# Summing the later adaLN columns on VectorE instead of TensorE in a hybrid decoder layer

## What is computed

```
mod = silu(c) @ w_ada + b_ada          # w_ada: 1024 x 6144
sh_m, sc_m, gt_m, sh_f, sc_f, gt_f = split(mod, 6)
h = rmsnorm(x, norm_pre_mix) * (1 + sc_m) + sh_m
proj = h @ w_in                        # 1024 x 4168
o = concat(hgrn2(4 heads of proj), sparse attention(4 heads, top 128 of 512 keys by an indexer))
x = x + gt_m * rmsnorm(o @ w_out, norm_post_mix)
h = rmsnorm(x, norm_pre_ffn) * (1 + sc_f) + sh_f
gate, up = split(h @ w_ffn_in, 2)      # 1024 x 5632
x = x + gt_f * rmsnorm((silu(gate) * up) @ w_ffn_out, norm_post_ffn)
```

## Time and profile before

| | us |
|---|---|
| median of 3 runs (802.88 to 803.44) | 803.05 |
| profiled execution, its own time | 805.04 |
| its span, first to last instruction | 803.3 |
| busy: TensorE / VectorE / ScalarE | 758.8 / 408.1 / 283.4 |

### The profile page before, as it was taken

How to read it: one execution, slowest core, us unless ns; L and a number is a source line. 1 busy time by engine, 2 the same in 40 slices (tenths; PEclk the granted TensorE clock), 3 DMA queues, 4 the chain that set the end, 5 groups by cost and what they waited for, 6 DMA issues and landing times.

```text
span 803.3 us, 10163 instructions
## 1 busy us (share of the span) xinstructions
PE 758.8 (94%) x3554; PEld 584.6 (73%) x3554; DVE 408.1 (51%) x782; ACT 283.4 (35%) x463; POOL 11.4 (1%) x39
## 2 busy tenths in 40 slices
PE   4889999999999889998997999999999999999995
PEld 3555477777866576665885888888888888888884
DVE  3857669797988525427347332222333225344344
ACT  6345452534233233244257233322233333112123
POOL 5000000000000000000000000000000000000000
PEclk9899999999999989997998999999999999999998
DMA  9935015243343150552410432233333233423202
GB/s 310 347 88 150 1 45 167 73 136 102 106 134 107 28 179 19 165 204 84 160 50 27 131 100 84 80 102 104 104 104 91 77 94 123 139 80 103 78 1 105
DMA packets 103845, 88.02 MB, mean 110 GB/s; under 512 B 2980, under 2 KB 93192, under 8 KB 103816
## 3 DMA queue, kind: packets, MB, share of 16 engines
q1 hardware_dynamic: 103816, 87.65, 35.6%
HBM read 85.55 MB, written 2.10 MB: 109 GB/s over the span
## 4 chain that ended last, share of the span: by engine, by line
PE 84%; DVE 9%; issue 2%; DMA 2%; ACT 1%; SPq 1%; DVEq 0%; ACTq 0%
PE ps L1240 45%; PE ps L1261 21%; PE ps L1346 3%; PE ps L1453 2%; PE ps L1291 2%; PE ps L1521 1%; PE ps L1431 1%; DMA w_raw<-in_w_in 1%; DVE w_lo L779 1%; PE ps L1496 1%; PE ps L1580 1%; PE ps L1516 1%; PE ps L1588 1%; DVE score L1002 1%; DVE top L997 1%
## 5 line engine op out<-in xcount | busy, mean ns | idle before, releaser
L1240 PE MATMUL ps<-h_hi,w_hi 128*128 128x512 f32 x576 | 235.2, 408 | 1.1 <-DVE h_lo L832 1.1
L1240 PE MATMUL ps<-h_hi,w_lo 128*128 128x512 f32 x576 | 225.1, 391 | 0.0
L1240 PE MATMUL ps<-h_lo,w_hi 128*128 128x512 f32 x576 | 225.0, 391 | 0.0
L779 DVE TENSOR_TENSOR w_lo<-w_raw,w_hi 128x1024 fp32r<-128x1024 f32 (+1 forms) x110 | 128.7, 1187 | 168.8 <-ACT w_hi L434 168.6
L434 ACT ACTIVATE w_hi<-w_raw 128x1024 fp32r<-128x1024 f32 (+1 forms) x110 | 110.5, 1026 | 97.4 <-PE ps L1261 91.7
L1240 PEld LDWEIGHTS ps<-h_hi,w_hi 128*128 128x128 f32 x576 | 108.5, 188 | 43.5 <-issue 21.7
L1240 PEld LDWEIGHTS ps<-h_hi,w_lo 128*128 128x128 f32 x576 | 108.4, 188 | 23.6
L1240 PEld LDWEIGHTS ps<-h_lo,w_hi 128*128 128x128 f32 x576 | 108.7, 189 | 20.5 <-issue 1.0
L1261 PE MATMUL ps<-w_hi,h_hi 128*128 128x512 f32 x240 | 94.8, 395 | 0.8 <-DVE mix L1138 0.8
L1261 PE MATMUL ps<-w_lo,h_hi 128*128 128x512 f32 x240 | 94.0, 392 | 0.0
L1261 PE MATMUL ps<-w_hi,h_lo 128*128 128x512 f32 x240 | 93.9, 391 | 0.0
(11 more groups left out here) (223 smaller groups left out, 696.6 us busy)
## 6 DMA issues: line engine op xcount, KB each, us to landing
w_raw<-in_w_ffn_in SPq DMA_DIRECT2D x44, 512.0 KB, 4.0
w_raw<-in_w_in SPq DMA_DIRECT2D x28, 512.0 KB, 6.4
w_raw<-in_w_ffn_out SPq DMA_DIRECT2D x22, 512.0 KB, 3.6
adaw<-in_w_ada SPq DMA_DIRECT2D x20, 512.0 KB, 5.0
act<-in_w_ada SPq DMA_DIRECT2D x12, 512.0 KB, 9.0
res<-in_x SPq DMA_DIRECT2D x8, 512.0 KB, 4.8
adaw<-in_w_ada SPq DMA_DIRECT2D x4, 1024.0 KB, 5.3
act<-in_w_ada SPq DMA_DIRECT2D x4, 1024.0 KB, 5.2
```

What stands on the lines that cost most here:

```text
L779: V.tensor_tensor(w_lo[slot][:, 0:n], w_raw[slot][:, 0:n], w_hi[slot][:, 0:n].bitcast(f32), ALU.subtract).then_inc(lo_ok, 1)
L1240: last = mm(ps[bank][0:rows, :], a, b, start=(k == 0 and n == 0), stop=(k == KT - 1 and n == 2))
```

## The change

The sum over the 1024 rows is taken apart. VectorE holds a running total of 128 partitions x 1024 columns for each later block. For row block k (128 rows, one per partition) it adds w_ada[k rows, 1024 columns] times silu(c) of these rows, a per-partition scalar (scalar_tensor_tensor). After eight adds, the total only has to be summed over partitions, which TensorE does with ones: for the gates one matmul of ones with the total both sums and spreads (gate_rows), for shift and scale 16 small ones make columns (ffn_sums).

- HGRN2 heads: halves, sums, copies and bias adds are gone.
- Attention heads 0, 1, 2: VectorE does eight adds each, for gt_m, sh_f, sc_f: two at t = 2, two after the last normalise, four after the copy of the output to mix. Loads are 1 MB (two row blocks), in two slots; twelve in all.
- The diagonals with L1135, L1588, L702 and the wait of head 1 for them are gone. The bias of a gate is loaded into row 0 of the total, which POOL has zeroed; the post-norm gains are loaded spread over all partitions instead of with the small parameters (two small loads fewer at the start).
- Attention head 3: ahead of its output matmuls TensorE does gate_rows for gt_m and ffn_sums; VectorE multiplies the gates by the gain.
- FFN: gt_f is summed in passes 0 to 7, one 512 KB load and one add each (add_tail), the loop of passes is cut in two, and gate_rows stand before the last pass.

The core of the diff:

```
@@ SP
-            load_gates_ada(0, 0)
...
-            load_norm_ada(3, 1)
+            def load_sum(n):
+                col = (2, 3, 4)[n // 4] * D_MODEL
+                if n == 0:
+                    sp.wait_ge(ada_used, START_ADA)
+                elif n == 1:
                     sp.wait_ge(o_mm, HG_HEADS)
                 else:
+                    sp.wait_ge(sum_used, 2 * n - 2)
+                sp.dma_start(sum_slot[n % 2].rearrange("p (k n) -> p k n", k=2),
+                             w_ada_k[:, 2 * (n % 4):2 * (n % 4) + 2, col:col + D_MODEL]).then_inc(sum_loaded[n % 2], 16)
+            def load_tail(k):
+                wait_apart(sum_used, k + SUMS)
+                sp.dma_start(tail_slot, w_ada[0][ds(k * P, P), 5 * D_MODEL:6 * D_MODEL]).then_inc(tail_loaded, 16)
...
+            with sp.Fori(0, KT) as i:
+                load_fin(i)
+                load_tail(i)
+            with sp.Fori(KT, FT // 2) as i:
+                load_fin(i)
@@ VectorE
+            def add_sum(h, n):
+                ve.wait_ge(sum_loaded[n // 2 % 2], h * 32 + 16 * (n // 4 + 1))
+                w = sum_slot[n // 2 % 2][:, n % 2 * D_MODEL:(n % 2 + 1) * D_MODEL]
+                silu = silu_pad[:, n * 32:n * 32 + 1]
+                first_head = isinstance(h, int)
+                total = sum_gate_mix if first_head else act[:, ds(h * D_MODEL, D_MODEL)]
+                if n == 0 and first_head:
+                    ve.wait_ge(mix_bias, 16)
+                else:
+                    ve.wait_ge(sum_used, h * KT + n)
+                if n == 0 and not first_head:
+                    V.tensor_scalar(total, w, silu, None, ALU.mult).then_inc(sum_used, 1)
+                else:
+                    V.scalar_tensor_tensor(out=total, in0=w, scalar=silu, in1=total, op0=ALU.mult,
+                                           op1=ALU.add).then_inc(sum_used, 1)
+            def add_tail(k):
+                ve.wait_ge(tail_loaded, k * 16 + 16)
+                V.tensor_copy(silu_k[:, :], silu_pad[:, ds(k * 32, 1)]).then_inc(tail_k, 1)
+                ve.wait_ge(tail_k, k + 1)
+                ve.wait_ge(sum_used, k + SUMS)
+                V.scalar_tensor_tensor(out=sum_gate_ffn, in0=tail_slot, scalar=silu_k[:, :], in1=sum_gate_ffn,
+                                       op0=ALU.mult, op1=ALU.add).then_inc(sum_used, 1)
@@ VectorE, att_body
+                    if not last and t == 2:
+                        add_sum(h, 0)
+                        add_sum(h, 1)
+                    if not last and t == 2:
                         split_lo(h * 3 + (G_ATT + 5), 2)
                 normalise(TT - 1)
                 if not last:
+                    add_sum(h, 2)
+                    add_sum(h, 3)
+                if not last:
                     split_lo(h * 3 + (G_ATT + 6), 0)
-                adaln_set(h)
-                if first:
...
-                    for n in range(2 * KT):
-                        V.tensor_scalar(diag[:, n * P:(n + 1) * P], ident[:, :], gate_cols[:, n:n + 1], None,
-                                        ALU.mult).then_inc(diag_ok, 1)
+                if last:
+                    ve.wait_ge(post_loaded, 32)
+                    for b in range(2):
+                        ve.wait_ge(gate_mm, b + 1)
+                        V.tensor_tensor(gate_mix[:, b * SEQ:(b + 1) * SEQ], ps[2 + b][:, :],
+                                        gate_mix[:, b * SEQ:(b + 1) * SEQ], ALU.mult).then_inc(gate_ok, 1)
+                    ve.wait_ge(ada_sum, 1)
+                    V.tensor_tensor(mod[:, 24:40], ps[6][:, 0:16], prm[:, 24:40], ALU.add).then_inc(mod_ok, 1)
                 ve.wait_ge(pv_mm, h * 4 + 4)
                 V.tensor_copy(mix[:, ds(h * SEQ + HG_HEADS * SEQ, SEQ)], ps[7][:, :]).then_inc(att_out, 1)
+                if not last:
+                    for n in range(4, KT):
+                        add_sum(h, n)
@@ TensorE
-                        ada_half(5, st // 2, adaw)
-                    elif st == 7:
-                        te.wait_ge(rows_ok, h + 1)
-                        ada_sums(5)
...
+            def gate_rows(total, bank, b):
+                mm(ps[bank + b][:, :], ones[:, :], total[:, b * SEQ:(b + 1) * SEQ], start=True,
+                   stop=True).then_inc(gate_mm, 1)
+            def ffn_sums():
+                for n in range(2 * KT):
+                    total = (sum_shift, sum_scale)[n // KT]
+                    last = mm(ps[6][:, n:n + 1], total[:, n % KT * P:(n % KT + 1) * P], ones[:, 0:1], start=True,
+                              stop=True)
                 last.then_inc(ada_sum, 1)
@@ TensorE, att_body
                 if not first:
-                    te.wait_ge(gate_ok, 4)
-                    te.wait_ge(mod_ok, h + (HG_HEADS + 1))
+                    te.wait_ge(v_ok, h)
                 partner(0, aq)
...
                 fill(20, 24)
+                if last:
+                    te.wait_ge(sum_used, SUMS)
+                    te.wait_ge(lg_ok, TT * ATT_HEADS)
+                    gate_rows(sum_gate_mix, 2, 0)
+                    gate_rows(sum_gate_mix, 2, 1)
+                    ffn_sums()
                 for t in range(TT):
-                    if t == TT - 1:
-                        te.wait_ge(rows_ok, h + (HG_HEADS + 1))
-                        ada_sums(6)
@@ TensorE, FFN
+            te.wait_ge(sum_used, SUMS + KT)
+            gate_rows(sum_gate_ffn, 4, 0)
+            gate_rows(sum_gate_ffn, 4, 1)
             fin_pass(FT // 2 - 1, False, True)
```

More of the change, by code:

```diff
@@ L171, in build @@
         small = sem("small")
[L172 removed]
+        sum_loaded, sum_used = [sem(f"sum_loaded{n}") for n in range(2)], sem("sum_used")
+        mix_zero, ffn_zero, mix_bias, ffn_bias = (sem(n) for n in ("mix_zero", "ffn_zero", "mix_bias", "ffn_bias"))
+        post_loaded, tail_loaded, tail_k = sem("post_loaded"), sem("tail_loaded"), sem("tail_k")
         ada_used, mod_ok, scale_ok = sem("ada_used"), sem("mod_ok"), sem("scale_ok")
@@ L290, in load_out @@
                 load_rows(w_out, k, k % 4)
[L292 to L305, removed]
+            w_ada_k = w_ada[0].rearrange("(k p) n -> p k n", p=P)
+            def load_sum(n):
[3 more added lines that the diff above has]
+                elif n == 1:
                     sp.wait_ge(o_mm, HG_HEADS)
                 else:
[L308 to L311, removed]
+                    sp.wait_ge(sum_used, 2 * n - 2)
[4 more added lines that the diff above has]
+                sp.dma_start(tail_slot, w_ada[0][ds(k * P, P), 5 * D_MODEL:6 * D_MODEL]).then_inc(tail_loaded, 16)
             for j in range(4):
                 load_hg(0, j)
-            load_gates_ada(0, 0)
             load_hg(1, 0)
@@ L697, in _ @@
             att_body(0, False)
-            for n in range(4):
-                sc.wait_ge(gate_mm, 4 * n + 4)
-                dst = (gate_mix if n < 2 else gate_ffn)[:, (n % 2) * SEQ:(n % 2 + 1) * SEQ]
-                sc.activation(dst, ps[(2, 3, 4, 6)[n]][:, :], ACT.Copy).then_inc(gate_ok, 1)
             with sc.Fori(1, ATT_HEADS - 1) as h:
@@ L1119, in att_body @@
                         split_lo(G_OUT + 1 + t, 1 + t)
-                    elif not last and t == 2:
+                    if not last and t == 2:
+                        add_sum(h, 0)
+                        add_sum(h, 1)
+                    if not last and t == 2:
                         split_lo(h * 3 + (G_ATT + 5), 2)
@@ L1190, in _ @@
                     swiglu(i, v)
+            ve.wait_ge(ffn_bias, 16)
+            with ve.Fori(0, KT) as i:
+                fin_pass(i)
+                add_tail(i)
+            with ve.Fori(KT, FT // 2 - 1) as i:
+                fin_pass(i)
             def split_act(k, slot):
@@ L1206, in _ @@
             swiglu(FT // 2 - 1, 0)
+            for b in range(2):
+                ve.wait_ge(gate_mm, b + 3)
+                V.tensor_tensor(gate_ffn[:, b * SEQ:(b + 1) * SEQ], ps[4 + b][:, :],
+                                gate_ffn[:, b * SEQ:(b + 1) * SEQ], ALU.mult).then_inc(gate_ok, 1)
             ve.wait_ge(act_ok[0], 2)
@@ L1394, in att_project @@
                     feature_step(k, j, 1 - j % 2)
-            def ada_sums(bank):
-                for c in range(4):
-                    last = mm(ps[bank][:, c:c + 1], ada_rows[:, c * P:(c + 1) * P], ones[:, 0:1], start=True, stop=True)
+            def gate_rows(total, bank, b):
[6 more added lines that the diff above has]
+                              stop=True)
                 last.then_inc(ada_sum, 1)
@@ L1584, in _ @@
             att_body(0, True, False)
-            te.wait_ge(mod_ok, HG_HEADS + 2)
-            te.wait_ge(diag_ok, 16)
-            for n in range(16):
-                mm(ps[(2, 3, 4, 6)[n // 4]][:, (n % 4) * P:(n % 4 + 1) * P], ones[:, :], diag[:, n * P:(n + 1) * P],
-                   start=True, stop=True).then_inc(gate_mm, 1)
             with te.Fori(1, ATT_HEADS - 1) as h:
```

116 lines of the change are left out of this document (51 added, 65 removed).

## The result

| | before | after |
|---|---|---|
| median of 5 runs, us (lowest to highest) | 803.44 (802.88 to 804.71) | 807.71 (807.39 to 809.61) |
| profiled execution, us | 805.04 | 807.42 |
| its span | 803.3 | 805.7 |
| its mean granted clock | 0.976 | 0.965 |

The ratio after to before is 1.0055, 95% interval 1.0039 to 1.007: slower, by little. Since an interval from a few runs can mislead (experiment 12), a wider comparison helps: all five runs of the change, 807.39 or more, lie above each of the 56 runs of the kernel before that this study has (800.4 to 807.08). The forecast was 805.4. From span to span it said +2.4 and +2.4 came; from median to median +4.3 came.

The account below looks back on a forecast made before the run. TensorE was taken to bound the kernel, with 84% of the chain of waits. Terms of -24.4 and +26.8 us net +2.4; with the profile-to-median difference carried over from the 803.05 median, forecast 805.4, range 798.5 to 811.

Parts of the forecast that it names:

- HGRN2 heads: Removing TensorE's halves and sums there, 11.2 us of work, gives back only 4.5 us (bounds 2 and 11.2).
- rival B: The halves come out of the HGRN2 heads in full, 11.2 us instead of 4.5: 798.7 us; chance 0.07.
- Diagonals and halves: Dropping the diagonals after head 0 saves 10.3 us; dropping halves and sums in attention heads 0 to 2 saves 8.4.
- Price of an add: A VectorE add takes 1.28 us, spaced 1.39 in head 0, 1.50 in the loop; boundary delays 5.2, 5.5, 5.0, together +15.6.
- Rival C: Waits among the adds cost nothing, spacing 1.15 us, so boundaries cost 12.8 instead of 15.6: 802.6 us; chance 0.12.
- Clock at the boundaries: TensorE's idle of about 6 us after heads 0 and 1 lowers its clock: +5.6 us; third boundary -0.9.
- Rival A: The clock holds, if idle at a boundary stays under about 2.7 us: -5.6, 799.8 us; chance 0.16.
- Last head: Gate rows and 16 column sums ahead of attention head 3's output matmuls cost +3.7 us net (bounds 3 and 4.4).
- From span to median: The profiled execution's 2.0 us above the median 803.05 is carried over, so net +2.4 gives 805.4 us.
- Loads, FFN adds: Loads arrive without a wait; FFN tail adds lie in VectorE's idle time, costing nothing; FFN gate rows cost +1.9 us.
- D: Loads come late: adds 6 and 7 wait 2 to 3 us in three heads, +6 to +9, about 812 us; chance 0.12.
- E: The adds are hidden, TensorE not waiting for the rope, so no boundary or clock cost: 784 us; chance 0.03.

Follow-up runs that it names:

- experiment 12: The kernel before, unchanged, profiled a second time: 805.45 us, ratio 1.0029 (1.0006 to 1.0051) against itself.
- experiment 1: Changed kernel with all four late adds of attention heads 0 to 2 issued ahead of the output copy instead of behind it: 790.62 us, ratio 0.9818.
- experiment 6: On the kernel of experiment 1, each of the 16 sums over partitions takes 32 columns of ones instead of one, same result: 788.28 us, ratio 0.9808.
- experiment 4: Changed kernel with 128 columns instead of one per sum over partitions in the last head, FFN shift and scale wrong: 804.4 us, ratio 0.9992.
- experiment 9: On the kernel of experiment 1, only the first of the 16 sums over partitions is made, result wrong: 786.34 us, ratio 0.9789.

## Why the prediction was right, and where a term was off

*HGRN2 heads: right.* -5.0 against -4.5. The waits moved from VectorE to TensorE as forecast (2.4 us for L1031 before, about 9 expected):

```profile
PE ps L1495 <- DVE act L1061: 7.1, 10, 2.0
PE ps L1502 <- DVE act L1061: 1.1, 1, 1.1
```

TensorE's 11.2 us of halves and sums gave 5; rival B, all of it, is out.

*Diagonals and halves: right.* Head 1's partner follows head 0's output matmuls with no gap (281.17 above). The stretch gave 2.1 us more than -13.1; some 1.7 of that is the clock in head 0, below.

*Price of an add: right in length, too high in spacing.* Two take 2.60 us: 1.28 each, spaced 1.31 in the loop and 1.39 in head 0, not 1.50. The gap of 0.26 beside a register wait was not the model for these. The delays were 5.0, 5.0 and 4.4 (idle 5.58 - 0.58, 5.51 - 0.59, 7.80 - 3.43) instead of 5.2, 5.5 and 5.0. The Trainium skill (VectorE: DVE Perf Modes, The DRAIN you can't avoid) says that a semaphore after each operation costs nothing extra; 0.03 us in the loop is close to that, 0.11 in head 0 is not. Rival C, the outcome by that rule, had a spacing of 1.15, and that is out too.

*Clock at the boundaries: right in kind, a little high in size.* It fell at all three. Low-clock work lasted 6.3, 7.1 and 6.8 us. With delays of 5.0 us each and 2.8 us of halves and sum gone, the table leaves 2.2 and 2.4 us for the clock in heads 1 and 2, where 2.8 stood each time. Rival A is out, and its condition was wrong too: it had the clock hold if the idle time stays under about 2.7 us, and experiment 1 shows it falling behind 1.39. The windows behind the first gap:

```profile
288.00:292.00 4.00, 2.62 (x4) 0.89 (x5) 1.90 (x4) 0.00 (x0) 0.00 (x0) 0.60 1.01 369
292.00:296.00 4.00, 4.00 (x12) 3.20 (x12) 2.41 (x4) 0.00 (x0) 0.00 (x0) 0.55 0.69 265
296.00:300.00 4.00, 4.00 (x19) 2.76 (x17) 3.21 (x14) 1.47 (x5) 0.00 (x0) 1.00 0.42 118
```

*Clock in head 0: not foreseen.* The same stretch of idle time, 2.69 us, stands in head 0 of both kernels. Before, the clock fell behind it; in the profile after it did not:

```profile
265.00:269.00 4.00, 4.00 (x20) 3.26 (x19) 3.42 (x4) 2.08 (x4) 0.00 (x0) 1.00 0.01 2
269.00:273.00 4.00, 4.00 (x20) 3.25 (x19) 3.54 (x9) 1.77 (x6) 0.00 (x0) 1.00 0.93 292
```

Over the 14 profiles of this study, all with this idle stretch, it fell in 8 and held in 6. The prediction took one fall for a rule ("all three stretches told of above, 2.69 us and more, fell"). The Trainium skill (TensorE: Matmul & The Clock Gate, Part 1) says of the matmuls at low clock at the start of a kernel that their number varies between runs of one kernel. These profiles show such variation in mid-kernel too: behind this stretch the clock was low for 3.4 us in five, for 6.8 in three and not at all in six.

*Last head: mis-sized, +6.6 where +2.8 stood* (3.7 less the 0.9 given back at the boundary), *and +1.6 behind it where nothing stood.* The term "16 sums are 4 x 0.79" = 3.16 us counted only the instructions at the price of the old sums. Even at full clock 32 such records take about 3.5 us (experiment 6: 362.97 to 366.46). Here they took 4.1 (374.74 to 378.86), because the clock fell inside them; the output matmuls behind them took 4.61 us against 2.40 (experiment 4), and the first eight matmuls of the output projection followed each other every 0.43 us instead of every 0.23, which is the +1.6. The waits of TensorE for w_lo, 0.98 and 0.29 us, used up most of what the missing halves gave. Experiment 4 shows the cause; experiment 9 leaves the exact size open.

*From span to median: wrong.* The 2.0 us by which the profiled execution of before lay above its median was carried over. It is no fixed overhead: every run lies 1.7 us above its span, and that execution was one of those with a lower clock (0.976). The five runs of the change all sat at 0.963 to 0.965, and its profiled execution lay 0.3 below its median. So the difference that the forecast carried over was not there, and 2 us of the 4.3 were missed. What makes the runs' clocks differ is open: head 0's is a part at most. From a mean of 0.976 to 0.986 it takes some 16 us less of low clock (an estimate: 0.010 of the 803 us, at half clock), and the stretch in head 0 had 3.4.

*Loads, FFN adds: right.* No add waited for a DMA; the FFN cost 1.4 against 1.9. Rivals D and E are out. What E would have been worth was there in part all the same: with the adds hidden the kernel ran 790.6, against E's 784. That 783.95 was reached with the sums spread as well is another edit's gain, and no match for E.

## What to carry to other kernels

Work that goes from the bounding engine to an idle one is priced by its place, not by its length: look at the idle time ahead of the instruction it is queued beside. Here 5.2 us of adds stood right behind 5.7 us of idle, and swapping the two was worth over 2% of the kernel.

Count a block of tiny matmuls with what follows it: check the granted clock behind it. If it falls, spreading the block among larger matmuls can shorten the low clock (10.2 us to 3.4 or none here), but look at more than one execution.

When a profiled execution differs from the median, look at its clock before carrying the difference over, and don't make a rule of a clock fall seen once behind a short idle stretch.

## What the runs showed of the hardware that I had not expected

The granted clock fell while TensorE was busy 1.00 of the time with matmuls of one column: to 0.50 within a block of 16 sums (32 records), in each of five profiles. With 128 columns the block of 32 records took 3.73 us instead of 4.25 to 4.75 and kept 1.00 (one profile); with 32 columns it kept 1.00 for one pass (one profile) and fell to 0.52 in the second pass of another.

From one to 128 moving columns these small sums cost TensorE nearly the same at full clock: 32 records took 3.65 us with 32 columns and 3.73 with 128, and ten records with one column took 1.17.

Behind an idle stretch of 2.69 us the clock fell in 8 of 14 profiles, and behind gaps of 1.25 to 1.75 us in 10 of 16 cases. Behind 0.58 and 0.59 us, in the kernel before, it held. So one profile of a kernel with such a gap doesn't tell what the next one will do.
